# Attention scores with the high and low halves of the keys stacked on the two row halves of the TensorE array

## The chip, the core and the metric

The kernel runs on one core of one Trainium2 chip. The time is the device time of one execution in microseconds, from the first to the last instruction with what lies around them; the shown times are those of repeated runs, and their median counts.

## What is computed

One inference step of a small hybrid network: 128 context tokens and 512 latent tokens of width 1024, two layers. Layer 0 mixes tokens by differential attention, layer 1 by a bidirectional mLSTM; each is followed by a gated ConvFFN. Everything is in 32 bit floats. The change lies in the attention, cut here to what matters (8 heads, two softmax maps m per head, d = DA_DK = 64):

```python
def diff_attend(q, k, v, lam):
    ...
        s = jnp.einsum('bqhmd,bkhmd->bhmqk', qi, k).astype(jnp.float32) * scale
        p = jax.nn.softmax(s, axis=-1)
        a = (p[:, :, 0] - lam * p[:, :, 1]).astype(v.dtype)
        return jnp.einsum('bhqk,bkhd->bqhd', a, v)
```

Context queries see the 128 context keys; latent queries see 128 cached keys and the 512 latent keys, which are rotated (rope) before, as the latent queries are.

## The kernel before

**Precision.** TensorE (PE) multiplies numbers of type fp32r, which are shorter than a float. So every operand is kept as a high part (a cast) and a low part (the float less the high part), and a product is the sum of three: high x high, high x low, low x high. Weights get their high part from ScalarE (ACT, line 1422) and their low part from GpSimd (POOL, line 593); activations get the low part from VectorE (DVE).

**Layout.** The query and key rows of a head are 2 x 64: map 0 on partitions 0 to 63, map 1 on 64 to 127. Qh, Ql (128 x 640: 128 context and 512 latent tokens) and Kh, Kl (128 x 768, with 128 cached keys behind) exist twice, for even and odd heads.

**Scores** (`scores`, L964 to L989). A head has five steps st = 0 to 4; step 0 is the context tile (i = 4), steps 1 to 4 are the four latent query tiles of 128 rows. A latent tile fills `psS`, three banks of 512 columns, with 640 scores of each map: spans of 128 and 512 keys for map 0, of 256 and 384 for map 1. Each span is three matmuls (Qh with Kh, Qh with Kl, Ql with Kh) of 64 rows, so a latent tile has twelve and the context tile six. The spans of 128 (map 0) and 384 (map 1) share a bank: PE waits on its own semaphore `sc_part` ahead of the latter. `psS` exists once: ahead of each tile PE waits for the exponentials of the tile before (`exp_ready`).

**The ring around a tile.** scores (PE) -> `nmax` (DVE: row maximum over psS, L2384, and a small product, L2386) -> `exps` (ACT, L1631) -> `combine` (DVE, L2394 to L2399) -> `turn` (PE: five transposes into psT) -> `turned` (ACT: high part, L1642; DVE: low part Al, L2410) -> values (PE). `psT` exists once too: it holds in turn the transposed tiles, the transposed values of a head (`turn_v`; split by ACT `values_hi` and DVE `values_lo`) and the sums of squares (`rms`, L1025 to L1029). The order in which it is used is a list (`_turn_uses`), and PE waits on `t_free` for the use before.

**The order on each engine** is written out by hand, one function `head` for each. PE puts pieces of the next projections (`qkv`, matmuls into `pj`, L765: pairs of 320 columns, in steps of two) between the attention's steps. At the end of head h PE does: scores(h, 4), 2 pieces, turn(h, 3), 2 pieces, turn_v(h), 2 pieces, rms(h-1) (only h > 0), 1 piece, values_ctx(h), 1 piece, scores(h+1, 0). `rms(h-1)` waits until `values_lo(h)` has freed psT. DVE at the end of head h does: nmax(h, 3), turned(h, 2), rotate("k", h+1), combine(h, 3), nmax(h, 4), turned(h, 3), q_lo(h+1), k_lo(h+1), values_lo(h), and then combine(h, 4). So the low parts of the next head's query and key stand between the last transposed tile and the values. ACT does in the middle of head h: exps(h, 2), q_hi(h+1) (L1668), unit_split(3h+5) (a weight's high part, L1422), turned(h, 2), exps(h, 3), cache_hi(h+1) (the cached keys and values), copy_kv (the value projection), k_hi(h+1) (L1677), turned(h, 3), exps(h, 4), values_hi(h), unit_split(3h+6). POOL's subtraction (L593) follows each unit_split.

The last head prepares no next one; PE fills its gaps with other work (`last_blocks`).

Of the kernel before, what the change touches and what calls it, by code (L numbers as in the profile page):

```python
# [14 lines left out]
P = 128  # L15
# [106 lines left out]
QT = (4, 0, 1, 2, 3)  # L122

# [60 lines left out]
def hybrid_step(nc, a, o):  # L184

    ctx = ExitStack()
    with ctx:
# [62 lines left out]
        with ExitStack() as s:  # L250
# [4 lines left out]
            Qh, Ql, Kh, Kl = ([] for _ in range(4))  # L255
            with ExitStack() as g:
                lwq = sb("lwq", [P, 2, 512], F32, g)
            for k in range(2):
                Qh.append(sb(f"Qh{k}", [P, TP], F32R, s))
                Ql.append(sb(f"Ql{k}", [P, TP], F32R, s))  # L260
            with ExitStack() as g:
                lwk = sb("lwk", [P, 2, 512], F32, g)
            for k in range(2):
                Kh.append(sb(f"Kh{k}", [P, KW], F32R, s))
                Kl.append(sb(f"Kl{k}", [P, KW], F32R, s))
# [9 lines left out]
            ckv = sb("ckv", [P, 2, P], F32, s)  # L275
            sm = sb("sm", [P, 16], F32, s)
            lam = sb("lam", [P, 8], F32, s)
            lamp = sb("lamp", [P, 2, DK], F32, s)
# [462 lines left out]
        def _(pe):  # L741
# [222 lines left out]
            def scores(h, st):  # L964

                idx, par, i = 5 * h + st, h % 2, QT[st]
                if idx > 0:
                    pe.wait_ge(exp_ready, idx)
                if idx == 1:
                    pe.wait_ge(mods_ready, 1)  # L970
                if i == 4:
                    pe.wait_ge(qk_ready, 2 * h + 2)
                    spans = [(0, C0, C0 + CTX, 0), (640, C0, C0 + CTX, 1)]
                    q0 = C0
                else:


                    spans = [(512, L0 + 512, KW, 0), (0, L0, L0 + 512, 0), (1024, L0 + 384, KW, 1), (640, L0, L0 + 384, 1)]
                    q0 = L0 + i * P
                for at, k0, k1, m in spans:  # L980
                    r = slice(DK * m, DK * (m + 1))
                    if i < 4 and at == 640:
                        pe.wait_ge(sc_part, 4 * h + i + 1)
                    for n, (q, kk) in enumerate(((Qh, Kh), (Qh, Kl), (Ql, Kh))):
                        last = mm(psS[:, at:at + k1 - k0], q[par][r, q0:q0 + P], kk[par][r, k0:k1],  # L985
                                  start=(n == 0), stop=(n == 2))
                    if i < 4 and at == 512:
                        last.then_inc(sc_part, 1)
                last.then_inc(sc_done, 1)  # L989
# [423 lines left out]
        def _(act):  # L1413
# [234 lines left out]
            def copy_q(n):  # L1648
                if n > 0:
                    act.wait_ge(qk_ready, 2 * n - 1)  # L1650
                v = _qkv_unit("q", n)
                evac(v // 2, v % 2, h32[0][:, :])
# [13 lines left out]
            def q_hi(n):  # L1666
                act.wait_ge(roped, 2 * n + 1)
                nc.scalar.copy(Qh[n % 2][:, :], h32[0][:, :]).then_inc(qk_hi, 1)  # L1668

            def cache_hi(n):  # L1670
                act.wait_ge(ckv_in, 32 * (n + 1))
                nc.scalar.copy(Kh[n % 2][:, L0 + LAT:KW], ckv[:, 0, :])
                nc.scalar.copy(Vh[n % 2][:, 4, :], ckv[:, 1, :]).then_inc(ckc_hi, 1)

            def k_hi(n):
                act.wait_ge(roped, 2 * n + 2)
                nc.scalar.copy(Kh[n % 2][:, 0:L0 + LAT], h32[1][:, 0:L0 + LAT]).then_inc(qk_hi, 1)  # L1677
# [362 lines left out]
        def _(dve):  # L2040
# [387 lines left out]
            def q_lo(n):  # L2428
                dve.wait_ge(qk_hi, 2 * n + 1)
                tt(Ql[n % 2][:, :], h32[0][:, :], Qh[n % 2][:, :].bitcast(F32), ALU.subtract).then_inc(qk_ready, 1)  # L2430

            def k_lo(n):
                par = n % 2
                dve.wait_ge(ckc_hi, n + 1)
                tt(Kl[par][:, L0 + LAT:KW], ckv[:, 0, :], Kh[par][:, L0 + LAT:KW].bitcast(F32), ALU.subtract)
                tt(Vl[par][:, 4, :], ckv[:, 1, :], Vh[par][:, 4, :].bitcast(F32), ALU.subtract).then_inc(ck_split, 1)
                dve.wait_ge(qk_hi, 2 * n + 2)
                tt(Kl[par][:, 0:L0 + LAT], h32[1][:, 0:L0 + LAT], Kh[par][:, 0:L0 + LAT].bitcast(F32),
                   ALU.subtract).then_inc(qk_ready, 1)
# [457 lines left out]
```

## Time and profile before

| what | value |
|---|---|
| times of 3 runs | 1748.39 us median (1747.43 to 1749.07) |
| profiled execution | 1748.54 us, span from first to last instruction 1746.8 us |
| mean granted TensorE clock | 0.994 of full speed |
| busy in the span | PE 97%, PE weight loads 91%, DVE 63%, ACT 40%, POOL 36% |
| score matmuls (L985) | 432, first at 58.8 us, last at 340.4 us |

The profile's page gives the busy time of each engine; the attention is the stretch from 58 to about 345 us. Matmuls are pipelined: the record of a matmul lasts longer than the array is occupied by it, so the spacing of starts tells its cost, and a busy PE isn't one at its peak. The chain of waits follows the work that ended last back through its releasers; a wait's releaser is inferred from semaphore events.

### The profile page before, as it was taken

The numbers are of one execution on the slowest core, as the hardware profiler recorded it, in microseconds if no ns is written. First come the engines' busy times: TensorE is split into PE (matmuls) and PEld (weight loads), VectorE is DVE, ScalarE is ACT, GpSimd is POOL, SyncE is SP. The second block draws the span as 40 slices with busy tenths as digits, with TensorE's granted clock in tenths as the row PEclk, the third lists the DMA queues.
The fourth block names the chain that finished last, engine by engine and source line by source line (L and its number), as shares of the span: only waits on it lengthen the run. The fifth ranks groups of instructions, "written<-read, shape, count | busy, mean of one in ns | idle before, by whom it ended". The sixth has DMA issues, their size and how long they took to land.

```text
span 1746.8 us, 30132 instructions
## 1 busy us (share of the span) xinstructions
PE 1696.8 (97%) x11450; PEld 1594.1 (91%) x11450; DVE 1097.0 (63%) x1775; ACT 696.4 (40%) x1134; POOL 631.4 (36%) x317
## 2 busy tenths in 40 slices
PE   7999999899999999999999999999999999999996
PEld 4888888598989999889998899998999999999996
DVE  4776777757876515767458554644878861487824
ACT  3455555527332212232246554554463331233324
POOL 2222111356442333323454222124745333333444
PEclk9999999999999999999999999999999999999998
DMA  9322222521444213543221112211212222222221
GB/s 358 136 65 73 62 62 81 207 85 46 190 176 161 97 57 121 183 181 129 83 70 55 64 55 75 71 49 49 91 37 72 72 90 69 70 72 72 86 84 60
DMA packets 59770, 170.97 MB, mean 98 GB/s; under 512 B 7945, under 2 KB 20489, under 8 KB 59665
## 3 DMA queue, kind: packets, MB, share of 16 engines
q1 hardware_dynamic: 51584, 163.33, 26.8%
q10 hardware_dynamic: 8080, 6.18, 1.1%
q8 instruction: 73, 1.20, 0.3%
q14 instruction: 33, 0.26, 0.0%
HBM read 161.07 MB, written 4.74 MB: 95 GB/s over the span
## 4 chain that ended last, share of the span: by engine, by line
PE 74%; DVE 9%; ACT 5%; POOL 4%; issue 4%; DVEq 3%; DMA 1%; ACTq 1%; SPq 0%; POOLq 0%
PE pj L765 58%; POOL wlo L623 3%; PE mO L1280 2%; ACT pr L1631 2%; PE psO L1020 2%; PE pfrow L790 1%; PE psS L985 1%; DVEq L2385 1%; PE st_va L765 1%; POOL ss L637 1%; DVE pr L2399 1%; PE mO L765 1%; PE st_mu L765 1%; DVE sm L2384 1%; PE mS L1236 1%
## 5 line engine op out<-in xcount | busy, mean ns | idle before, releaser
L593 POOL TENSOR_TENSOR wlo<-wraw,whi 128x1024 fp32r<-128x1024 f32 (+1 forms) x116 | 301.9, 2603 | 739.7 <-ACT whi L1422 739.7
L765 PE MATMUL pj<-Hh,whi 128*128 128x320 f32 x2192 | 521.3, 317 | 2.2 <-POOL wlo L623 0.9
L765 PE MATMUL pj<-Hh,wlo 128*128 128x320 f32 x2192 | 504.9, 309 | 0.0
L765 PE MATMUL pj<-Hl,whi 128*128 128x320 f32 x2192 | 502.7, 310 | 0.0
L765 PEld LDWEIGHTS pj<-Hh,whi 128*128 128x128 f32 x2192 | 364.8, 188 | 28.5 <-issue 22.8
L765 PEld LDWEIGHTS pj<-Hh,wlo 128*128 128x128 f32 x2192 | 368.1, 188 | 0.3
L765 PEld LDWEIGHTS pj<-Hl,whi 128*128 128x128 f32 x2192 | 367.5, 188 | 0.4
L1422 ACT CAST whi<-wraw 128x1024 fp32r<-128x1024 f32 (+1 forms) x168 | 187.2, 1114 | 265.2 <-PE pj L765 227.7
L2295 DVE SCALAR_TENSOR_TENSOR fcv<-fus,vec,fcv 128x127 f32<-128x127 f32 (+1 forms) x176 | 206.4, 1214 | 14.4 <-issue 13.8
L1428 ACT COPY fus<-pj 128x640 f32<-128x640 f32 x84 | 58.3, 696 | 382.9 <-PE pj L765 382.9
L2157 DVE SCALAR_TENSOR_TENSOR X<-pj,mods,X 128x128 f32<-128x128 f32 (+5 forms) x114 | 43.1, 434 | 207.4 <-PE pj L765 207.3
L765 PE MATMUL pj<-Gh,whi 128*128 128x320 f32 x704 | 168.4, 310 | 0.8 <-POOL wlo L623 0.8
L765 PE MATMUL pj<-Gh,wlo 128*128 128x320 f32 x704 | 167.4, 308 | 0.0
L765 PE MATMUL pj<-Gl,whi 128*128 128x320 f32 x704 | 167.3, 308 | 0.0
L2298 DVE SCALAR_TENSOR_TENSOR fcv<-fus,vec,fcv 128x127 f32<-128x127 f32 (+1 forms) x176 | 129.1, 774 | 14.4 <-issue 13.8
L2292 DVE TENSOR_SCALAR fcv<-fus,vec 128x640 f32<-128x640 f32 x88 | 61.0, 694 | 111.7 <-ACT fus L1428 111.7
L668 POOL TENSOR_TENSOR wlo<-wraw,whi 128x1024 fp32r<-128x1024 f32 x27 | 68.4, 2534 | 148.7 <-ACT whi L1422 142.1
L765 PEld LDWEIGHTS pj<-Gh,whi 128*128 128x128 f32 x704 | 119.4, 188 | 1.6 <-POOL wlo L623 1.3
L623 POOL TENSOR_TENSOR wlo<-wraw,whi 128x1408 fp32r<-128x1408 f32 (+2 forms) x28 | 85.4, 3049 | 97.4 <-ACT whi L1422 92.9
L765 PEld LDWEIGHTS pj<-Gh,wlo 128*128 128x128 f32 x704 | 119.4, 188 | 0.3
L765 PEld LDWEIGHTS pj<-Gl,whi 128*128 128x128 f32 x704 | 119.5, 188 | 0.0
L2384 DVE TENSOR_REDUCE sm<-psS 128x2 f32<-128x1280 f32 (+1 forms) x40 | 50.9, 1274 | 31.0 <-PE psS L985 30.9
(374 smaller groups left out, 2414.2 us busy)
## 6 DMA issues: line engine op xcount, KB each, us to landing
wraw<-in_w_up SPq DMA_DIRECT2D x84, 512.0 KB, 3.5
fwr<-in_w_ada SPq DMA_DIRECT2D x56, 512.0 KB, 5.7
wraw<-in_w_dn SPq DMA_DIRECT2D x32, 704.0 KB, 4.1
wraw<-in_w_qkv SPq DMA_DIRECT2D x24, 512.0 KB, 3.5
wraw<-in_w_mlin SPq DMA_DIRECT2D x24, 512.0 KB, 3.4
awr<-in_w_ada SPq DMA_DIRECT2D x16, 512.0 KB, 10.4
awr<-in_w_ada SPq DMA_DIRECT2D x16, 256.0 KB, 7.9
wraw<-in_w_wo SPq DMA_DIRECT2D x8, 512.0 KB, 3.5
```

The costliest lines, as they stand in the source:

```text
L593: nc.gpsimd.tensor_tensor(wlo[k][:, 0:width], wraw[k][:, 0:width], whi[k][:, 0:width].bitcast(F32), ALU.subtract).then_inc(w_lo, 1)
L623: nc.gpsimd.tensor_tensor(wlo[k][:, c0:width], wraw[k][:, c0:width], whi[k][:, c0:width].bitcast(F32), ALU.subtract).then_inc(w_lo, 1)
L668: nc.gpsimd.tensor_tensor(wlo[v % 2][:, 0:width], wraw[v % 2][:, 0:width], whi[v % 2][:, 0:width].bitcast(F32), ALU.subtract).then_inc(w_l ...
L765: last = mm(out[:, c, 0:HALF], w, x[:, j, c * HALF:(c + 1) * HALF], start=(j == 0 and n == 0), stop=(j == n_k - 1 and n == 2))
L1020: last = mm(psO[:, :], v_[par][:, c, :], t_[:, c, :], start=(c == 0 and n == 0), stop=(c == 4 and n == 2))
L1422: nc.scalar.copy(whi[k][:, 0:width], wraw[k][:, 0:width]).then_inc(w_hi, 1)
L1428: nc.scalar.copy(dst.rearrange("p (a b) -> p a b", a=2), src[:, :, 0:HALF]).then_inc(pj_copied, 1)
L2157: last = stt(out=x, in0=src[:, bank, c0:c1], scalar=gt, in1=x, op0=ALU.mult, op1=ALU.add)
L2292: ts(c[:, :], f[:, :], tap[1], bias, ALU.mult, ALU.add)
L2295: stt(out=c[:, t0 + 1:t1], in0=f[:, t0:t1 - 1], scalar=tap[0], in1=c[:, t0 + 1:t1], op0=ALU.mult, op1=ALU.add)
L2298: last = stt(out=c[:, t0:t1 - 1], in0=f[:, t0 + 1:t1], scalar=tap[2], in1=c[:, t0:t1 - 1], op0=ALU.mult, op1=ALU.add)
L2384: nc.vector.tensor_reduce(sm[:, 0:2], s_, AX.X, ALU.max)
```

## The change

The scores get a contraction over all 128 rows of the array. For each map m there is now a key tile `Ks[m]` with the high part on the map's own 64 partitions (`OWN[m]`) and the low part on the other 64 (`OTHER[m]`), and a query tile `Qd[m]` with the query's high part on both halves. One `stacked` matmul then gives high x high + high x low; `low_query` (64 rows, the map's own) adds low x high. A latent tile has four of each, in the order tail, right (stacked), tail, right (low), wide (stacked), the wait on `sc_part`, left (stacked), left, wide (low); the context tile has two of each.

The halves have to be written: `q_hi` makes four passes of 64 partitions for one of 128 (two on the own half, then the semaphore `qk_hi`, then two across to the other half), `k_hi` and the keys of `cache_hi` two for one on ACT; `q_lo`, and both subtractions of keys in `k_lo` (writing across to the other half), two for one on DVE. `Ql` exists once and not twice, `Qd` four times; `ckv` and `lamp` lie in unused columns of the weight buffers. `copy_q` waits for the key's low part of the head before, and not the query's.

```diff
--- before.py
+++ after.py
+OWN = (slice(0, DK), slice(DK, 2 * DK))
+OTHER = OWN[::-1]
...
-            Qh, Ql, Kh, Kl = ([] for _ in range(4))
+            Qd, Ks = [], []
...
-                Qh.append(sb(f"Qh{k}", [P, TP], F32R, s))
-                Ql.append(sb(f"Ql{k}", [P, TP], F32R, s))
+                Qd.append([sb(f"Qd{k}{m}", [P, TP], F32R, s) for m in range(2)])
+                if k == 0:
+                    Ql = sb("Ql", [P, TP], F32R, s)
...
-                Kh.append(sb(f"Kh{k}", [P, KW], F32R, s))
-                Kl.append(sb(f"Kl{k}", [P, KW], F32R, s))
+                Ks.append([sb(f"Ks{k}{m}", [P, KW], F32R, s) for m in range(2)])
...
-            ckv = sb("ckv", [P, 2, P], F32, s)
+            ckv = wraw[1][:, D:D + 2 * P].rearrange("p (a k) -> p a k", a=2)
...
-            lamp = sb("lamp", [P, 2, DK], F32, s)
+            lamp = wraw[0][:, D:D + 2 * DK].rearrange("p (a k) -> p a k", a=2)
...
                 if i == 4:
                     pe.wait_ge(qk_ready, 2 * h + 2)
-                    spans = [(0, C0, C0 + CTX, 0), (640, C0, C0 + CTX, 1)]
-                    q0 = C0
+                q0 = C0 if i == 4 else L0 + i * P
+
+                def stacked(at, k0, k1, m):
+                    mm(psS[:, at:at + k1 - k0], Qd[par][m][:, q0:q0 + P], Ks[par][m][:, k0:k1], start=True, stop=False)
+
+                def low_query(at, k0, k1, m):
+                    return mm(psS[:, at:at + k1 - k0], Ql[OWN[m], q0:q0 + P], Ks[par][m][OWN[m], k0:k1], start=False, stop=True)
+
+                if i == 4:
+                    first, second = ((640 * m, C0, C0 + CTX, m) for m in range(2))
+                    stacked(*first)
+                    stacked(*second)
+                    low_query(*first)
+                    last = low_query(*second)
                 else:
-
-
-                    spans = [(512, L0 + 512, KW, 0), (0, L0, L0 + 512, 0), (1024, L0 + 384, KW, 1), (640, L0, L0 + 384, 1)]
-                    q0 = L0 + i * P
-                for at, k0, k1, m in spans:
-                    r = slice(DK * m, DK * (m + 1))
-                    if i < 4 and at == 640:
-                        pe.wait_ge(sc_part, 4 * h + i + 1)
-                    for n, (q, kk) in enumerate(((Qh, Kh), (Qh, Kl), (Ql, Kh))):
-                        last = mm(psS[:, at:at + k1 - k0], q[par][r, q0:q0 + P], kk[par][r, k0:k1],
-                                  start=(n == 0), stop=(n == 2))
-                    if i < 4 and at == 512:
-                        last.then_inc(sc_part, 1)
+                    wide, tail = (0, L0, L0 + 512, 0), (512, L0 + 512, KW, 0)
+                    left, right = (640, L0, L0 + 384, 1), (1024, L0 + 384, KW, 1)
+                    stacked(*tail)
+                    stacked(*right)
+                    low_query(*tail).then_inc(sc_part, 1)
+                    low_query(*right)
+                    stacked(*wide)
+                    pe.wait_ge(sc_part, 4 * h + i + 1)
+                    stacked(*left)
+                    low_query(*left)
+                    last = low_query(*wide)
                 last.then_inc(sc_done, 1)
...
             def copy_q(n):
                 if n > 0:
-                    act.wait_ge(qk_ready, 2 * n - 1)
+                    act.wait_ge(qk_ready, 2 * n)
                 v = _qkv_unit("q", n)
                 evac(v // 2, v % 2, h32[0][:, :])
...
             def q_hi(n):
                 act.wait_ge(roped, 2 * n + 1)
-                nc.scalar.copy(Qh[n % 2][:, :], h32[0][:, :]).then_inc(qk_hi, 1)
+                for m in range(2):
+                    last = nc.scalar.copy(Qd[n % 2][m][OWN[m], :], h32[0][OWN[m], :])
+                last.then_inc(qk_hi, 1)
+                for m in range(2):
+                    nc.scalar.copy(Qd[n % 2][m][OTHER[m], :], h32[0][OWN[m], :])
             def cache_hi(n):
                 act.wait_ge(ckv_in, 32 * (n + 1))
-                nc.scalar.copy(Kh[n % 2][:, L0 + LAT:KW], ckv[:, 0, :])
+                for m in range(2):
+                    nc.scalar.copy(Ks[n % 2][m][OWN[m], L0 + LAT:KW], ckv[OWN[m], 0, :])
                 nc.scalar.copy(Vh[n % 2][:, 4, :], ckv[:, 1, :]).then_inc(ckc_hi, 1)
             def k_hi(n):
                 act.wait_ge(roped, 2 * n + 2)
-                nc.scalar.copy(Kh[n % 2][:, 0:L0 + LAT], h32[1][:, 0:L0 + LAT]).then_inc(qk_hi, 1)
+                for m in range(2):
+                    last = nc.scalar.copy(Ks[n % 2][m][OWN[m], 0:L0 + LAT], h32[1][OWN[m], 0:L0 + LAT])
+                last.then_inc(qk_hi, 1)
             def values_hi(h):
                 act.wait_ge(t_full, USE["v", h] + 1)
...
             def q_lo(n):
                 dve.wait_ge(qk_hi, 2 * n + 1)
-                tt(Ql[n % 2][:, :], h32[0][:, :], Qh[n % 2][:, :].bitcast(F32), ALU.subtract).then_inc(qk_ready, 1)
+                for m in range(2):
+                    r = OWN[m]
+                    last = tt(Ql[r, :], h32[0][r, :], Qd[n % 2][m][r, :].bitcast(F32), ALU.subtract)
+                last.then_inc(qk_ready, 1)
             def k_lo(n):
                 par = n % 2
                 dve.wait_ge(ckc_hi, n + 1)
-                tt(Kl[par][:, L0 + LAT:KW], ckv[:, 0, :], Kh[par][:, L0 + LAT:KW].bitcast(F32), ALU.subtract)
+                for m in range(2):
+                    k_, r = Ks[par][m], OWN[m]
+                    tt(k_[OTHER[m], L0 + LAT:KW], ckv[r, 0, :], k_[r, L0 + LAT:KW].bitcast(F32), ALU.subtract)
                 tt(Vl[par][:, 4, :], ckv[:, 1, :], Vh[par][:, 4, :].bitcast(F32), ALU.subtract).then_inc(ck_split, 1)
                 dve.wait_ge(qk_hi, 2 * n + 2)
-                tt(Kl[par][:, 0:L0 + LAT], h32[1][:, 0:L0 + LAT], Kh[par][:, 0:L0 + LAT].bitcast(F32),
-                   ALU.subtract).then_inc(qk_ready, 1)
+                for m in range(2):
+                    k_, r = Ks[par][m], OWN[m]
+                    last = tt(k_[OTHER[m], 0:L0 + LAT], h32[1][r, 0:L0 + LAT], k_[r, 0:L0 + LAT].bitcast(F32), ALU.subtract)
+                last.then_inc(qk_ready, 1)
```

## Rows read from the trace of the kernel before

**Rows 1.** Windows: stretch, its length, busy us (instructions) by engine, granted clock, DMA
```profile
172.00:210.00 38.00, 37.68 (x256) 33.39 (x256) 27.71 (x48) 20.89 (x43) 7.56 (x4) 1.00 0.22 65
```
**Rows 2.** Chain of waits, head 3: start us, length us, what
```profile
191.22 1.43 PE psS L985 x10
...
195.91 0.82 DVE Al L2410
...
197.87 0.74 DVE Kl L2438
...
199.55 1.31 PE psT L1028 x4
```
**Rows 3.** List of waits, 58 to 350 us: total us, times, longest us
```profile
PE psT L1028 <- DVE Vl L2446: 1.0, 6, 0.2
```
**Rows 4.** Timeline of PE, scores(3, 1): start, length, line, out<-in, count
```profile
172.41 0.39 PE L1020 MATMUL psO<-Ah,Vl 128*128 128x512 f32 x1
172.73 0.32 PE L985 MATMUL psS<-Kh,Qh 64*128 64x128 f32 x1
172.89 0.27 PE L985 MATMUL psS<-Kl,Qh 64*128 64x128 f32 x1
...
173.01 0.55 PE L985 MATMUL psS<-Kh,Qh 64*128 64x256 f32 x2
...
173.83 0.33 PE L985 MATMUL psS<-Kh,Ql 64*128 64x384 f32 x1
174.09 0.55 PE L765 MATMUL pj<-Hh,whi 128*128 128x320 f32 x2
174.48 0.45 PE L765 MATMUL pj<-Hh,wlo 128*128 128x320 f32 x2
174.78 0.45 PE L765 MATMUL pj<-Hl,whi 128*128 128x320 f32 x2
```
**Rows 5.** Groups by line and shape, 55 to 350 us: busy us, mean ns
```profile
L2430 DVE TENSOR_TENSOR Ql<-h32t,Qh 128x640 fp32r<-128x640 f32 x7 | 5.7, 816 | 0.0
```
**Rows 6.** The same view, 800 to 1000 us (the mLSTM's gates)
```profile
L2593 DVE TENSOR_TENSOR O32m<-O32m 36x640 f32<-36x640 f32 x1 | 0.8, 818 | 0.1
...
L1795 ACT ACTIVATE O32m<-mT,gbias 36x640 f32<-36x640 f32 x1 | 0.8, 799 | 0.0
```
**Rows 7.** Timelines of ACT, POOL, DVE and PE in head 3
```profile
185.24 0.72 ACT L1668 CAST Qh<-h32t 128x640 fp32r<-128x640 f32 x1
185.85 1.05 ACT L1422 CAST whi<-wraw 128x1024 fp32r<-128x1024 f32 x1
...
186.98 2.46 POOL L593 TENSOR_TENSOR wlo<-wraw,whi 128x1024 fp32r<-128x1024 f32 x1 [14.65 <-ACT whi L1422]
199.43 2.37 POOL L593 TENSOR_TENSOR wlo<-wraw,whi 128x1024 fp32r<-128x1024 f32 x1 [9.98 <-ACT whi L1422]
...
188.68 0.80 DVE L2386 TENSOR_SCALAR sm<-sm 128x2 f32<-128x2 f32 x1
...
190.12 0.68 DVE L2421 TENSOR_TENSOR sx<-sx,rope 128x512 f32<-128x512 f32 x1
...
193.19 0.89 DVE L2399 SCALAR_TENSOR_TENSOR pr<-pr,sm 128x640 f32<-128x640 f32 x1
...
194.44 0.71 PE L1001 MATMUL psT<-ident,pr 128*128 128x128 f32 x5
```
**Rows 8.** Timelines of DVE and POOL in the first ConvFFN
```profile
473.24 3.17 DVE L2295 SCALAR_TENSOR_TENSOR fcv<-fus,vec,fcv 128x127 f32<-128x127 f32 x2 [0.17 <-issue]
...
473.29 2.57 POOL L668 TENSOR_TENSOR wlo<-wraw,whi 128x1024 fp32r<-128x1024 f32 x1 [1.20 <-ACT whi L1422]
```
**Rows 9.** Timeline of PE, end of head 0
```profile
92.94 0.77 PE L1001 MATMUL psT<-ident,pr 128*128 128x128 f32 x5 [1.36 <-DVE pr L2399]
```
**Rows 10.** Windows, as rows 1, in the last head
```profile
324.00:325.70 1.70, 0.00 (x0) 0.00 (x0) 0.16 (x1) 1.66 (x4) 0.00 (x0) 1.00 0.92 320
328.00:332.00 4.00, 4.00 (x23) 1.61 (x20) 2.87 (x7) 3.06 (x7) 0.27 (x1) 0.57 0.56 213
```

## The prediction

> **What bounds the kernel now.** Counting matmuls would say: PE, the matmul engine. I first cut out the stage that the edit touches, the attention, with one stretch of the windows: in 38 us PE is busy for 37.68, VectorE (DVE) for 27.71, ScalarE (ACT) for 20.89 [rows 1]. A PE that is never idle beside two half idle engines still may not set the time alone, because the engines hand each tile around in a ring: scores, row maximum, exponential, combination, transposes. So second the chain of waits over one steady head, head 3. From the scores of step 1 on (174.2) it runs on DVE and ACT for 17 us, touches PE again at 191.22 for the scores of step 4, and comes back to DVE: the last transposed tile's low part (Al, 195.91), then Ql, Kl and Vl without a gap. PE's rms matmuls (199.55) can only follow Vl, and from there PE is the chain up to the next scores of step 1 [rows 2]. Third the list of waits: in six heads of eight these rms matmuls are released by Vl, up to 0.2 us after PE ran dry [rows 3]. So DVE has no slack between Al and Vl, and PE next to none before them. Two things matter: how long a score tile takes, and every microsecond of DVE between Al and Vl.
>
> **The score matmuls.** Twelve become eight, but the instruction stream shows what the twelve cost [rows 4]. The matmuls of map 0 (upper 64 rows of the array) and of map 1 (lower 64) already run beside each other: map 1's 256 columns start at 173.01, while map 0 is at work. Each half streams 3 x 640 = 1920 columns. Afterwards a stacked matmul takes the whole array, 1280 columns, and the low queries, which can still pair up, add max(128, 256) + max(512, 384) = 768: 2048. The saved third was hidden by the other half.
>
> Then the edges. The last full-array matmul ahead of the tile starts at 172.41 and lasts 0.23 by its columns (0.30 for twice 320 at 174.48), so the tile was due at 172.64. It comes at 172.73, and its second step 0.16 later where 0.11 is usual for weights of 128 columns: 0.15 to get in. The last score matmul (384 columns, 0.18) starts at 173.83 and leaves the array at 174.01; the projection starts at 174.09, and its second step comes 0.39 later against 0.30 for the third: 0.18 to get out. In all 172.64 to 174.19, 1.55 us. The new tile goes full, halves, full, halves, full: two such pairs of edges. In the spacings of rows 4: tail 0.11, right 0.12, in 0.15, pair 0.15, out 0.18, wide 0.23, left 0.18, in 0.15, pair 0.26, out 0.18, together 1.71: **0.16 us more per latent tile**, not less. Bounds: 0.13 less than now if the second pair of edges costs nothing, 0.4 more if the low queries run one after the other; I take 0.16, since both edges of the trace have the gap. The wait on sc_part is covered by the wide matmul, which stands between the short low query and it. The context tile changes three double steps for a stacked pair and a low pair between the same two edges: nothing, within 0.05.
>
> The Trainium skill says of this, in TensorEngine Tiling (Array Packing), Key Properties, that changing the tiling mode, and not just the tile, drains the array. By that rule the 0.33 us of edges is owed a second time, as I took it; if the gaps came from the semaphore wait ahead of the tile instead, the lower bound would hold, some 0.3 us per head less. The way out has no wait in front of it and shows the larger gap, so the trace sides with the rule.
>
> **The split of queries and keys.** Full-height instructions become pairs of half-height ones. Does a half cost half? A DVE subtraction of 128 x 640 takes 816 ns [rows 5], one of 36 x 640 takes 818, and an ACT pass of 36 x 640 takes 799 though it reads partitions from 64 on and writes them from 0 on [rows 6]. **Height is free, so each half costs the whole**, and the shift across partitions nothing on ACT; on DVE no row has one, and I take nothing too.
> DVE, between Al and Vl: one more Kl, 0.74, one more Ql, the same size, and one more cache part. From Al's end (195.91 + 0.82) to Kl (197.87) lie one Ql and two cache parts, 1.14, so a part is 0.20 [rows 2]. **1.67 us more on the chain in each head.**
> ACT: three more query passes and one more key pass, 0.61 apart (185.24 to 185.85 [rows 7]), and a cache pass of some 0.2: 2.6 us of an engine that idles 17 in 38. Key and cache passes lie in idle time ahead of turned(h, 3). The query passes stand ahead of the head's weight cast (185.85), which so comes 1.83 later, and with it GpSimd's subtraction (POOL), which starts 1.13 after the cast, and what DVE does beside it. PE needs those weights after the scores of step 4, 192.6, and has them at 191.4. The new wait of copy_q (2n for 2n - 1) is for a subtraction that ends before Vl, so before PE goes on: nothing. ckv and lamp move in memory and queue nowhere; the DMAs stay.
>
> **What DVE and POOL do to each other.** While POOL subtracts (2.4 us), DVE instructions from memory stand: L2386, on two numbers a row, takes 0.80 and ends with POOL [rows 7]. And where POOL comes while DVE works on a pair of them, it goes in between: POOL at 473.29, DVE's pair from 473.24 stretched to 3.17 [rows 8]. So I work out where POOL's two subtractions of a head fall.
> First: the chain behind step 1 is 0.16 later; four query passes from 185.40, the cast at 187.84, POOL 188.97 to 191.37. L2386 comes at 188.68 now, and 0.16 (the chain) to 0.32 (two score tiles in PE's order) later: 188.84 to 189.0, a tie; I take it as ahead. But then rotate("k") (L2421, 190.12) stands until 191.37 and its first step ends 1.2 late; the combination, done at 194.08 now, ends 195.3, and the transposes start at 195.35 in place of 194.44 [rows 7]: **Al is 0.9 us late**.
> Second: this POOL start follows the value transposes, which wait for Al: 199.43, 3.52 after Al [rows 2, 7]. The new order is Al, two Ql, two cache parts, V, two Kl; the second Kl would start 0.82 + 1.46 + 0.40 + 0.20 + 0.74 = 3.6 after Al. POOL comes during the first Kl and goes in between, as in rows 8. The second Kl is done at some 6.6, Vl at 7.5, and PE starts at 7.65 after Al where it is 3.64 now: **4.0 us late** in place of 1.67.
>
> **Sum.** A head with an rms behind it: 0.9 + 4.0 = 4.9 us, six of them: 29.4. Head 0 has no rms; PE there waits for the combination [rows 9], which already contains its POOL stall: of the 4.0 about 1.9 are left, 2.8 with the 0.9. The last head prepares nothing: two tiles on its chain, 0.3. The prologue's 1.67 lies under the 16 matmuls of ada_block(5) and the projection ahead of the first scores: nothing, or 1.7 once. Together 32.5 on the profiled execution's 1748.54 us (1746.8 span and 1.7 around it; the median of the runs is 1748.39): **1781 us**.
>
> **Rivals.**
> *POOL waits.* If the second Kl gets in ahead of POOL (0.1 us by my count), a head costs 0.9 + 1.67 = 2.6: six are 15.4, head 0 some 1.6, with the last head 17.3: 1766; with the lower bound of the tile 1762. Rows 8 speak against it.
> *L2386 is caught as well.* Then the exponentials of step 3 wait until 191.4, the scores of step 4 start at 193.2 and Al comes 2.1 late: 1.2 more in seven heads, 1789. The tie of rows 7 decides.
> *The clock falls.* PE stands some 4 us per head in the forecast. In the last head it stands from 324 to 325.7, and over the 4 us from 328 on the granted clock is 0.57, a mean of the levels 1.2 and 2.4 GHz: 4 x 0.43 = 1.7 us of PE lost [rows 10]. At 1.5 each in six heads 1790, with the former 1798. Against it: in steady heads PE's work on either side of the gap is dense.
> *It does what it says.* A half costs half, so DVE adds nothing, and the tile loses a third of its 1.43 us (172.73 to 174.16), 0.48, at two places of the chain: 0.96 x 7 = 6.7 less, 1742. The price of a half-height DVE instruction decides: at x of a full one DVE adds (2x - 1) x 1.67, and the gain lives below x = 0.79. Rows 6 say x = 1; then even a full third leaves 0.7 us a head too much, 1753.
>
> **Chances.** Forecast 0.38, POOL waits 0.20, L2386 caught 0.17, the clock (with or without that) 0.12, it does what it says 0.04; 0.04 for within 0.2% (3.5 us, about what a measurement tells from no change), with x in between; 0.05 for the 1753. The range takes in all but the ends: 1758 to 1799. Faster 0.04, same 0.04, slower 0.92.
>
> **What would show it.** Right: Ql and Kl halves of 0.82 us each; PE's gap ahead of L1028 grown from 0.2 to some 4 us, released by Vl; a second Kl of 3 us beside POOL; a head's first POOL start 2 us later after its scores; score tiles of 1.6 to 1.7 us with gaps of 0.1 inside. Wrong: halves of 0.4 us; score tiles near 1.0; a PE that goes into rms without a wait.

## The result

The changed kernel takes 1797.43 us (median of 4 runs, 1796.47 to 1797.93), the kernel before beside it 1748.08: a ratio of 1.0285, 95% interval 1.0273 to 1.0297. It is slower by 49 us; the forecast was slower by 32.5. The profiled span is 1796.2 us against 1746.8, and the difference arises in the attention: each head takes some 7.6 us more from one rms to the next, and the last rms of the attention comes 51.6 us later (405.70 against 354.14). Some 2 us come back behind it, 1.5 of them where the kernel before runs at a granted clock of 0.83 from 1190 to 1200 us; this profile has 1.00 over the same work, 1240 to 1250.

The windows of the changed kernel, columns as in [rows 1], over a stretch of the same length:

```profile
172.00:210.00 38.00, 33.36 (x193) 28.76 (x194) 25.06 (x43) 18.63 (x36) 5.22 (x2) 0.91 0.16 48
```
PE was busy for 37.68 there; now it stands for 4.6 us, and what it does runs at a granted clock of 0.91. The list of waits from 58 to 420 us (total, times, longest):

```profile
PE psT L1041 <- DVE Vl L2473: 27.8, 6, 4.6
PE psT L1014 <- DVE pr L2419: 3.8, 8, 1.2
PE psO L1024 <- DVE Vl L2473: 3.7, 1, 3.7
```
The first line is that of [rows 3], 1.0 us in six heads before, 27.8 now. The third is head 0, which has no rms: there the values of the context tile wait for Vl.

The timelines of DVE, POOL and PE at the end of head 3 (compare [rows 2, 7]):

```profile
218.07 0.83 DVE L2430 TENSOR_TENSOR Al<-psT,Ah 128x640 fp32r<-128x640 f32 x1
218.81 1.64 DVE L2452 TENSOR_TENSOR Ql<-h32t,Qd 64x640 fp32r<-64x640 f32 x2
220.49 0.59 DVE L2460 TENSOR_TENSOR Ks<-wraw,Ks 64x128 fp32r<-64x128 f32 x2
...
221.41 3.70 DVE L2465 TENSOR_TENSOR Ks<-h32t,Ks 64x640 fp32r<-64x640 f32 x2
225.14 0.69 DVE L2472 TENSOR_TENSOR Vl<-psT,Vh 128x512 fp32r<-128x512 f32 x1
...
221.60 2.84 POOL L596 TENSOR_TENSOR wlo<-wraw,whi 128x1024 fp32r<-128x1024 f32 x1 [8.94 <-ACT whi L1435]
...
226.18 1.82 PE L1041 MATMUL psT<-ss,ones 128*128 128x320 f32 x4 [4.63 <-DVE Vl L2473]
```
The two halves of the key are one group of 3.70 us: 0.82 for the first, then POOL up to 224.44, then the second. The rms follows Al by 8.11 us, where it was 3.64 [rows 2].

The groups by line and shape over 58 to 410 us (busy us, mean ns), against [rows 5, 6]:

```profile
L2465 DVE TENSOR_TENSOR Ks<-h32t,Ks 64x640 fp32r<-64x640 f32 x14 | 25.8, 1844 | 0.3
L2452 DVE TENSOR_TENSOR Ql<-h32t,Qd 64x640 fp32r<-64x640 f32 x14 | 11.4, 815 | 0.1
L1682 ACT CAST Qd<-h32t 64x640 fp32r<-64x640 f32 x14 | 10.1, 720 | 0.1
```
A half takes 815 ns on DVE, a whole 816; 720 ns on ACT, a whole 0.72 us [rows 7]. The 1844 is the mean of halves with and without POOL in between.

PE's timeline over a latent tile, as [rows 4]:

```profile
193.13 0.39 PE L1033 MATMUL psO<-Ah,Vl 128*128 128x512 f32 x1
193.36 0.39 PE L979 MATMUL psS<-Ks,Qd 128*128 128x128 f32 x2
193.68 0.38 PE L982 MATMUL psS<-Ks,Ql 64*128 64x128 f32 x2
194.00 0.67 PE L979 MATMUL psS<-Ks,Qd 128*128 128x512 f32 x2
194.60 0.50 PE L982 MATMUL psS<-Ks,Ql 64*128 64x384 f32 x2
195.03 0.56 PE L768 MATMUL pj<-Hh,whi 128*128 128x320 f32 x2
195.42 0.46 PE L768 MATMUL pj<-Hh,wlo 128*128 128x320 f32 x2
```
From its start to the next projection it takes 1.67 us, against 1.36 before (172.73 to 174.09). From the last matmul ahead of it, which takes in the way into the tile, it is 1.90 (193.13 to 195.03) against 1.68 (172.41 to 174.09): 0.22 us more.

The windows of 1 us behind the gap:

```profile
225.00:226.00 1.00, 0.00 (x0) 0.00 (x0) 0.97 (x4) 0.00 (x0) 0.00 (x0) 1.00 0.62 111
226.00:227.00 1.00, 0.82 (x3) 0.69 (x4) 0.85 (x5) 0.00 (x0) 0.00 (x0) 0.93 0.88 348
227.00:228.00 1.00, 1.00 (x3) 0.61 (x3) 0.76 (x1) 0.00 (x0) 0.00 (x0) 0.50 0.17 66
...
230.00:231.00 1.00, 1.00 (x7) 1.00 (x7) 0.00 (x0) 0.27 (x1) 0.00 (x0) 0.87 0.00 0
```
After 4.6 us without a matmul the clock stands at 0.50 for three microseconds, the lower of the two levels, 1.2 GHz for 2.4: 1.7 us of PE lost in this head (0.07 + 3 x 0.50 + 0.13).

### The profile page after: what moved, and what is told of

The parts are those of the page before. It is cut to its first block, busy times and chain, and to the rows that moved or that the text cites. A ratio compares the mean times of both kernels' runs of the same rounds, so it can differ in the third digit from the quotient of the medians.

```text
span 1796.2 us, 29908 instructions
## 1 busy us (share of the span) xinstructions
PE 1717.1 (96%) x11306; PEld 1598.5 (89%) x11306; DVE 1123.5 (63%) x1799; ACT 722.9 (40%) x1174; POOL 632.4 (35%) x317
## 4 chain that ended last, share of the span: by engine, by line
PE 74%; DVE 8%; ACT 5%; POOL 4%; issue 4%; DVEq 3%; DMA 1%; ACTq 1%; SPq 0%; POOLq 0%
PE pj L768 59%; POOL wlo L626 3%; PE mO L1293 2%; PE psO L1033 2%; PE pfrow L793 1%; DVEq L2415 1%; PE st_va L768 1%; POOL ss L640 1%; PE psS L979 1%; PE psT L1041 1%; PE psS L982 1%; PE mO L768 1%; PE st_mu L768 1%; ACT whi L1435 1%; PE mS L1249 1%
## 5 line engine op out<-in xcount | busy, mean ns | idle before, releaser
L2315 DVE SCALAR_TENSOR_TENSOR fcv<-fus,vec,fcv 128x127 f32<-128x127 f32 (+1 forms) x176 | 205.7, 1209 | 14.9 <-issue 14.3
L2318 DVE SCALAR_TENSOR_TENSOR fcv<-fus,vec,fcv 128x127 f32<-128x127 f32 (+1 forms) x176 | 134.5, 805 | 14.3 <-issue 13.7
## 6 DMA issues: line engine op xcount, KB each, us to landing
awr<-in_w_ada SPq DMA_DIRECT2D x16, 512.0 KB, 10.3
```

The source lines that it names most:

```text
L2315: stt(out=c[:, t0 + 1:t1], in0=f[:, t0:t1 - 1], scalar=tap[0], in1=c[:, t0 + 1:t1], op0=ALU.mult, op1=ALU.add)
L2318: last = stt(out=c[:, t0:t1 - 1], in0=f[:, t0 + 1:t1], scalar=tap[2], in1=c[:, t0:t1 - 1], op0=ALU.mult, op1=ALU.add)
```

## The experiments

All ratios are to the kernel before, run beside each on the same chip (medians 1746.7 to 1747.1 us). First come the parts, then the mechanism, then its price. "Period" is the time from one head's rms to the next in a steady head: 36.7 us before, 44.1 to 44.9 in the changed kernel (mean 44.4).

### The tile alone

```diff
-                for m in range(2):
-                    last = nc.scalar.copy(Qd[n % 2][m][OWN[m], :], h32[0][OWN[m], :])
-                last.then_inc(qk_hi, 1)
-                for m in range(2):
-                    nc.scalar.copy(Qd[n % 2][m][OTHER[m], :], h32[0][OWN[m], :])
+                nc.scalar.copy(Qd[n % 2][0][:, :], h32[0][:, :]).then_inc(qk_hi, 1)
...
```
The same for the keys and on DVE: every split is one whole-height instruction again, the eight matmuls stay.

> The eight matmuls of a tile as in the changed kernel, but queries and keys split by one full-height instruction each, as before the change; the scores are then not the reference's (map 1 multiplies the query's high part with the key's low part). Theory 'the splits cost it': a latent tile is 0.16 to 0.2 us longer than before, twice on the chain of a head and once or twice more in PE's order, so 1749.5 to 1753 us. Rival 'the tile gains, the splits hide it': a third of the matmuls gone shows, 1741 to 1746. Rival 'the tile costs it': the edges between full array and halves are worth most of the 49 us, over 1770.

Measured: 1751.94 us (1749.48 to 1755.12), ratio 1.0026, interval 1.0015 to 1.0037; a period of 37.25 us, and the clock at 1.00 up to the last head. So the eight matmuls by themselves gain nothing: they cost 0.6 us a head. From the last matmul ahead of a tile to the next projection, the tiles of steps 1 to 3 take 1.89, 1.96 and 2.03 us, against 1.68, 1.75 and 1.75 before; that of step 4, ahead of which PE stood for the exponentials before, takes 1.97 against 1.95.

### The splits alone

```diff
+                    for n, q in enumerate((Qd[par][m], Qd[par][m], Ql)):
+                        last = mm(psS[:, at:at + k1 - k0], q[r, q0:q0 + P], Ks[par][m][r, k0:k1], start=(n == 0), stop=(n == 2))
```
The twelve 64-row matmuls again, on the new tiles, whose halves are written as in the changed kernel.

> The half-height splits of the changed kernel, but twelve matmuls of 64 rows a tile, in the order before the change (the second of a span reads the key's high part once more in place of the low part, so the scores are not the reference's). Theory 'the splits cost it': nearly all of the 49 us stays, 1793 to 1797. Rival 'the tile costs it': 1750 to 1765. If the tile gains, more than the changed kernel's 1797.4.

Measured: 1796.17 us, ratio 1.0277 (1.0253 to 1.0301), and the same wait of PE as in the changed kernel, 27.8 us in six heads, 4.6 the longest. The loss is the splits.

### Halves on one engine only

ScalarE's copies in halves, VectorE's whole:

```diff
+                for m in range(2):
+                    last = nc.scalar.copy(Ks[n % 2][0][OWN[m], 0:L0 + LAT], h32[1][OWN[m], 0:L0 + LAT])
...
+                tt(Ks[par][1][:, 0:L0 + LAT], h32[1][:, 0:L0 + LAT], Ks[par][0][:, 0:L0 + LAT].bitcast(F32),
+                   ALU.subtract).then_inc(qk_ready, 1)
```

> The kernel of the tile alone (VectorE's splits whole) with ScalarE's copies in halves as the changed kernel has them: two halves and two more for the query, two for the key, two for the cached keys; both halves of the high key go to one tile and VectorE's whole-height difference to the other, so the scores are not the reference's. It splits the cost of the halves between the two engines. Theory A (VectorE's sequence ahead of Vl is the main cost, ScalarE only makes Al some 1.4 us late per head): 1751.9 + 6 x 1.4 = 1760 us, range 1756 to 1766, no idle stretch over 1 us ahead of rms, the clock 1.00. Theory B (ScalarE's halves carry half the loss or more, through Ah, the casts and POOL): 1772 us or more.

VectorE's in halves, ScalarE's whole:

```diff
+                for m in range(2):
+                    k_, r = Ks[par], OWN[m]
+                    last = tt(k_[1][r, 0:L0 + LAT], h32[1][r, 0:L0 + LAT], k_[0][r, 0:L0 + LAT].bitcast(F32), ALU.subtract)
```

> The kernel of the tile alone with VectorE's three low parts in halves (query, cached keys, keys: two instructions of 64 rows each in place of one of 128), ScalarE's copies whole. Each half stays on its own rows, where the changed kernel moves the key's halves to the other rows; the scores are not the reference's. Theory A (the two engines' halves add up, and what counts on VectorE is that two halves take twice the time of the whole and let POOL's split in between; the move to other rows costs nothing by itself): what ScalarE's halves do not explain, 1797.4 - (1758.2 - 1751.9) = 1791 us, range 1785 to 1796, with rms 8.1 us behind Al and 4.6 us of PE idle ahead of it. Theory B (the move across the rows, or the meeting of both engines' halves, is what costs): 1775 us or less, with the two key halves 1.65 us together.

Measured: ScalarE's halves 1758.15 us (ratio 1.0057, 1.0042 to 1.0072), as expected; a period of 38.06, 0.8 above the tile alone, and the rms 3.64 us behind Al as before. VectorE's halves 1797.5 us (1.0283, 1.0266 to 1.03), as much as the whole change. So VectorE's halves carry the loss, 45.6 us over the tile alone, and the expectation that the two add up (1791) was wrong by 6: ScalarE's 6 us are there only when VectorE's halves are not. Their timeline shows the same key halves, though here no half moves to other rows:

```profile
220.12 3.69 DVE L2458 TENSOR_TENSOR Ks<-h32t,Ks 64x640 fp32r<-64x640 f32 x2
223.85 0.69 DVE L2465 TENSOR_TENSOR Vl<-psT,Vh 128x512 fp32r<-128x512 f32 x1
```
The move to other rows costs nothing. Why the two engines' shares don't add shows in the stretches of a head. From the tile of step 1 to Al of step 4 it takes 23.91 us here and 24.71 in the changed kernel, so ScalarE's halves do make Al 0.8 us later there too. But from the rms to the next tile of step 1 it takes 12.0 to 12.7 us here, against 11.3 to 12.1: behind the gap of head 3 the granted clock is 0.50 from 224 to 230 us here, in the changed kernel from 227 to 230. What Al wins, the low clock takes back; why it falls earlier here is not shown.

### POOL waits, and PE kept busy

```diff
+                if v % 3 == 0 and v >= 6:
+                    pool.wait_ge(qk_ready, 2 * (v // 3))
+                split_one(v, D)
```

> The changed kernel, with GpSimd's second weight subtraction of a head waiting until the next head's key is split (one wait more on GpSimd, nothing else). Theory: the second Kl half (start to Vl 2.88 us) stands behind GpSimd; it falls to 0.85, rms starts some 6.1 us after Al in place of 8.1, 2.0 in six heads: 1785; if the shorter gap leaves PE's clock up, another 1.5 in each: 1776. Rival 'writing across the halves is what makes the second Kl slow': it keeps its length and the time stays at 1797.

Measured: 1774.88 us (1.0156, 1.013 to 1.0181), 22.5 us less and close to the 1776 of the theory with the clock; a period of 40.47 us, the rms 6.06 us behind Al, PE's wait 2.6 us a head, the clock at 1.00 but for one window. The timelines of DVE, POOL and PE:

```profile
210.91 1.65 DVE L2468 TENSOR_TENSOR Ks<-h32t,Ks 64x640 fp32r<-64x640 f32 x2
...
213.62 1.38 DVE L2419 TENSOR_TENSOR sm<-sm,lam 128x1 f32<-128x1 f32 x1
...
215.54 0.88 DVE L2422 SCALAR_TENSOR_TENSOR pr<-pr,sm 128x640 f32<-128x640 f32 x1
...
212.64 2.35 POOL L671 TENSOR_TENSOR wlo<-wraw,whi 128x1024 fp32r<-128x1024 f32 x1 [10.49 <-DVE Ks L2468]
...
217.38 0.77 PE L1017 MATMUL psT<-ident,pr 128*128 128x128 f32 x5
```
The two key halves take 1.65, so 2.0 of the 3.70 us were POOL's. The split now catches the next two-operand step of DVE, the product ahead of `pr`, and there it costs nothing: pr is done at 216.4, and PE comes to its transposes at 217.4. From the rms to the tile of step 1 it is 9.70 us, as with the tile alone.

```diff
+                    pe.wait_ge(o_free, 2 * h)
+                    for _ in range(18):
+                        mm(psO[:, :], Hh[:, 0, 0:P], Hh[:, 0, 0:512], start=True, stop=True)
```
This puts 18 matmuls of no use into PE's gap ahead of rms, in the changed kernel.

> The changed kernel, with 18 more matmuls of 512 columns (4.1 us, into a bank that is overwritten later) in PE's gap ahead of rms. Theory: the gap of 4.6 us is followed by about 3.5 us at a granted clock of 0.5, worth 1.7 us in each of six heads; with the gap filled the clock stays at 1.00: 1786 to 1788. Rival 'the low clock lies beside other waits and costs nothing': 1797.

Measured: from head 2 on the clock is 1.00, a period is 42.57 us, and the last rms of the attention comes 10.3 us earlier: 1.7 us in six heads, what the windows above give for the clock. The time falls by less, to 1791.56 us (1788.42 to 1794.69; 1.0251, 1.0219 to 1.0283). The profiled run is the slower of the two, and 7 us of its lead on the changed kernel go behind the attention: 4.4 at 1040 to 1070 us, where PE waits 3.9 us for DVE in the mLSTM and its clock falls, and the 2 that the changed kernel's profile gets back. Why DVE is late there I didn't follow up.

### Where the halves stand

Only the place of one line is changed, then of one more:

```diff
                 q_lo(h + 1)
+                values_lo(h)
                 k_lo(h + 1)
-                values_lo(h)
```

> The changed kernel with one line moved: VectorE takes the low part of the values (two instructions, 0.69 and 0.28 us) between the query's low halves and the key's low halves, in place of behind the key's. No instruction is added or taken away. Theory A (the halves cost because they stand ahead of Vl, on which the matmul that overwrites psT waits; neither their own busy time nor their lateness matters): rms falls back to some 3.7 us behind Al of step 4 (8.1 in the changed kernel), the idle stretch of PE of 4.6 us goes, the low clock behind it goes with it (1.7 us), and head 0's 3.7 us too; a head from rms to rms 38.3 us in place of 44.5; 1797.4 - 6 x 6.2 - 3.7 = 1756 us, range 1751 to 1762. Theory B (the work only comes late elsewhere: the key's low halves then hold up the scores of the next head, or combine of step 4, by what was saved): at most a third of it comes back, 1783 to 1797 us.

```diff
                 k_hi(h + 1)
+                q_twice(h + 1)
                 turned(h, 3)
```
(`q_twice` is the second pair of copies of `q_hi`; head 0 keeps the old place.)

> The kernel with the values first, and one more thing moved: ScalarE makes the query's second copy (two halves, 1.46 us) behind the key's high halves, where it idled 1.28 us before Ah of step 4, in place of ahead of the cast that POOL's first split waits on and of Ah of step 3. Theory A (the 1.4 us from the scores to Al come from ScalarE's queue and from POOL's split meeting the rotation of the key because the cast ended late): Ah of step 3 comes some 1.4 us earlier, the rotation's first product takes 0.7 to 0.9 us in place of 1.68, a head takes 37.0 to 37.5 us; 1750 to 1754 us, what the tile alone took (1751.9). Theory B (the copy is not what makes Al late, or its new place delays Ah of step 4 by what was saved): as the kernel with the values first, within 3 us.

Measured: values first 1788.96 us (1.024, 1.0224 to 1.0255): my theory fell, 8.5 us came back and not 41. The gap ahead of rms is gone, and the waits of PE from 60 to 420 us say where it went:

```profile
PE psT L1014 <- DVE pr L2419: 10.6, 15, 1.1
PE psS L979 <- DVE Ks L2465: 10.4, 7, 2.7
```
PE reaches the next head's context scores some 3 us after the start of rms, and needs the key there; behind it, the transposes need pr. With the second copy moved too it is 1778.67 us (1.0175, 1.0161 to 1.0188): the rotation's first product takes 0.68 again (1.68 in the changed kernel), but a period is still 40.9 and not the 37.0 to 37.5 of theory A. Al comes no earlier, 24.95 us after the tile of step 1 against 24.69 with the values first: POOL's first split now catches the small product of step 3 (1.42 us for 0.17), and the copies in their new place stand ahead of Ah of step 4. What came back, by the trace, is the clock, 1.00 from head 3 on: from the rms to the next tile of step 1 it takes 12.4 us, with the values first 13.8 to 15.0. DVE and POOL in that kernel:

```profile
204.92 1.42 DVE L2411 TENSOR_SCALAR sm<-sm 128x2 f32<-128x2 f32 x1
...
203.91 2.40 POOL L596 TENSOR_TENSOR wlo<-wraw,whi 128x1024 fp32r<-128x1024 f32 x1 [15.77 <-ACT whi L1435]
...
216.90 2.67 DVE L2465 TENSOR_TENSOR Ks<-wraw,Ks 64x128 fp32r<-64x128 f32 x2
...
216.97 2.45 POOL L596 TENSOR_TENSOR wlo<-wraw,whi 128x1024 fp32r<-128x1024 f32 x1 [10.66 <-ACT whi L1435]
```
POOL's second split now catches the cached keys. Next, POOL's split is held there too, as above:

> The kernel with values first and the query's second copy moved, and POOL's second split of a head held until the key's low halves are done. Theory A (what is left of the loss there is the split that catches the low halves of the cached keys, 2.67 us in place of 0.6, and so makes the key late for the next head's context scores, on which PE waits 1.3 us, with the combination behind it 1.1 us later than before): the cached halves take 0.6, the waits of psS on Ks go, a head takes 38 to 38.8 us in place of 40.9; 1778.7 - 6 x 2.5 - 1 = 1763 us, range 1758 to 1768. Theory B (the held split comes too late for its matmuls, or the key's halves are late without the collision): 1774 us or more.

Measured: 1779.16 us (1.0188, 1.0171 to 1.0205), no gain: theory A fell again. The cached halves take 0.59, PE doesn't wait for the key but for 0.6 us once, and the collision has moved on once more:

```profile
217.16 2.18 DVE L2424 TENSOR_TENSOR sm<-sm,lam 128x1 f32<-128x1 f32 x1
219.27 0.54 DVE L2425 TENSOR_SCALAR pr<-pr,sm 128x640 f32<-128x640 f32 x1
...
216.97 2.36 POOL L671 TENSOR_TENSOR wlo<-wraw,whi 128x1024 fp32r<-128x1024 f32 x1 [13.24 <-DVE Ks L2473]
...
220.82 0.77 PE L1017 MATMUL psT<-ident,pr 128*128 128x128 f32 x5 [2.58 <-DVE pr L2427]
```
A product of 0.16 us takes 2.18, and PE stands 2.58 us for pr. So in this order the path isn't Al to Vl but Al to pr, and it is one unbroken sequence of DVE: where POOL comes into it, its end is 2 us later.

### The price of the collision

The kernel with both moved, and the kernel before, each with POOL's second split on 8 columns of 1024:

```diff
+                split_one(v, 8 if v % 3 == 0 and v >= 6 else D)
```

> The kernel with values first and the query's second copy moved, in which POOL's second split of each head works on 8 columns of the 1024 (so that the low part of that weight is stale, and the result is not the reference's): no POOL instruction of 2.4 us lies beside VectorE's low parts. It prices what the collision costs there. Theory A (the split costs the 2 us that it takes from VectorE's sequence from Al to pr of step 4 wherever it stands in it, since PE waits for the end of that sequence): the cached halves take 0.6, PE's waits on Ks and on pr behind rms go (2.4 us a head), 1778.7 - 7 x 2.2 = 1763 us, range 1759 to 1767. Theory B (the plain durations of the halves carry the loss, the collision is hidden beside PE's work): 1774 us or more.

> The kernel before with the same cut: POOL's second split of each head on 8 columns, the low part of that weight stale. In the kernel before this split catches L2396 behind the values' low parts (2.26 us in place of 0.16, at 199.55). Theory A (there it costs nothing, since pr ends at 203.2 and PE comes to its transposes at 203.4 anyway): the time of the kernel before within 0.2%, 1744 to 1750 us; with the run beside it, the split costs some 2 us a head in the changed kernel's order and none in that of before. Theory B (it costs 2 us a head in both): 1735 us or less.

Measured: 1762.78 us (1.0095, 1.0074 to 1.0117), 15.9 us less than with the split, 2.3 in each of seven heads, with a period of 38.80; and 1746.18 us (0.9996, 0.9986 to 1.0005), no change. The same POOL instruction costs 16 us beside the halves, in this order, and nothing in the kernel before. There, too, it stops DVE for 2 us, as its timeline shows:

```profile
199.55 2.26 DVE L2396 TENSOR_TENSOR sm<-sm,lam 128x1 f32<-128x1 f32 x1
...
202.35 0.88 DVE L2399 SCALAR_TENSOR_TENSOR pr<-pr,sm 128x640 f32<-128x640 f32 x1
...
203.37 0.77 PE L1001 MATMUL psT<-ident,pr 128*128 128x128 f32 x5
```
and without the split:

```profile
199.63 0.16 DVE L2397 TENSOR_TENSOR sm<-sm,lam 128x1 f32<-128x1 f32 x1
...
200.33 0.89 DVE L2400 SCALAR_TENSOR_TENSOR pr<-pr,sm 128x640 f32<-128x640 f32 x1
```
Before, pr ends at 203.2, and PE comes to its transposes at 203.4 on its own. POOL's 2.1 us used up the slack of that sequence to within 0.2 us, so the first added half had nowhere to go.

### The twelve matmuls in another order

The kernel before with the two maps' matmuls in turn, in the context tile too, nothing else:

```diff
+                    for n in range(3):
+                        done = term(n, *tail)
+                        term(n, *right)
+                    done.then_inc(sc_part, 1)
...
+                    for n in (1, 2):
+                        term(n, *left)
+                        last = term(n, *wide)
```

> The kernel before with only its twelve 64-row matmuls of a latent tile put in another order: those of the two maps in turn (three pairs tail beside right, then wide beside left), nothing else. In the kernel before the three of a map follow one another on the same row half. Theory A (two matmuls on different row halves run beside each other, as the two pairs of step 4 in the rows of before and the pairs in the changed kernel do, so that the interleaved order gains what the present one leaves): 0.1 to 0.2 us less a latent tile, 28 tiles, 2.8 to 5.6 us in all where PE sets the pace: 1741 to 1745 us. Theory B (the stretch around the scores is set by what PE does next or by the other engines, or the halves already overlap as far as they can): within 0.1%, 1745.5 to 1749 us.

Measured: 1746.44 us (1.0000, 0.9991 to 1.0009). A tile takes 1.32 us from its first score to the projection (185.69 to 187.01), against 1.35 in the kernel before (185.40 to 186.75): the halves overlapped already. No version that I ran beats the kernel before.

## Why the prediction was right, and where it was off

The time lies inside the range, close to its upper end. That end stood for the clock together with a caught L2386; the clock fell, L2386 was missed, and head 0, Al and the spacing of the halves made up the rest. The direction and the mechanism were forecast; that the number is still in the range is in part luck.

**The cause: right.** Vl released PE, the gap grew to 4.6 us (forecast some 4), POOL went in between the two key halves, the small product of [rows 7] was missed by POOL's first split (L2406 took 0.17) and the rotation was caught (L2441, 1.68).

**The tile: the sign right, the size and the place too small.** I had 0.16 us more per latent tile; it is 0.21 to 0.28 in steps 1 to 3, and nothing in step 4, where PE waited before. I let it count at two places of the chain in the last head and inside Al's lateness elsewhere. Alone it costs 5 us, 0.6 a head. The Trainium skill's rule that a change of the tiling mode drains the array (TensorEngine Tiling (Array Packing), Key Properties) agrees with the sign of this, as [rows 4] did.

**Height is free: right; two halves at the spacing of wholes: wrong.** I spaced the added Ql and Kl by 0.74, the step from one whole subtraction to the next. The two halves of a pair don't overlap at all: they take 1.64 together, and the next step starts 1.68 behind their start (218.81 to 220.49). ACT's pairs take 1.45, where I had 0.61 for each pass. So the first key half started 3.34 us behind Al and not 2.88. POOL came 3.53 behind it (forecast 3.52), and the rms 8.11 (forecast 7.65): the whole difference of 0.46 is this term.

**Al 0.9 us late: it was 1.4** (24.94 us from the last matmul ahead of the tile of step 1 to Al, 23.50 before). The four query passes take 2.96 us up to the weight's cast (206.16 to 209.12), and not 2.44: halves at the spacing of wholes once more. So POOL's first split, and the rotation that stands beside it, end some 0.5 us later than I counted. The passes also stand ahead of Ah of step 3 on ACT, as the chain of waits of the changed kernel shows:

```profile
206.27 0.61 ACT Qd L1682
206.89 0.72 ACT Qd L1682
207.64 0.72 ACT Qd L1685
208.38 0.73 ACT Qd L1685
209.12 1.05 ACT whi L1435
210.16 0.60 ACT Ah L1655
210.78 0.82 DVE Al L2430
```
I had counted ACT as idle for 17 us in 38 and didn't name this Ah. But its Al is done at 211.6, and POOL, for which the rotation stands, at 212.7:

```profile
211.53 1.68 DVE L2441 TENSOR_TENSOR sx<-sx,rope 128x512 f32<-128x512 f32 x1
...
210.24 2.42 POOL L596 TENSOR_TENSOR wlo<-wraw,whi 128x1024 fp32r<-128x1024 f32 x1 [17.21 <-ACT whi L1435]
```

**The clock: the step that failed.** I gave its fall a chance of 0.12, as "PE's work on either side of the gap is dense". It fell in every steady head and cost 1.7 us each (priced at 1.5): the run with PE kept busy had 10.3 us of it back at the end of the attention, of some 17 that were missing. It is the largest part of the miss. Dense work around the gap was no reason; [rows 10] was the case to go by.

**Head 0: sized from the wrong wait.** I took 2.8 us from the combination, where PE waited before [rows 9]. It now waits 3.7 us for Vl ahead of that, at the context values, with Al's lateness still to come on top: from its first score to the first score of head 1 it takes 38.7 us against 32.3, 6.4 more.

**POOL waits: a rival priced too low.** Made on purpose, it gives 1774.9 and not 1766. The collision that it moves to the product ahead of pr costs nothing there; what I had too small is the halves themselves: the rms comes 6.06 us behind Al and not 5.31 (3.64 + 1.67), and Al is later by the 0.5 above. One head also has a low clock (a period of 42.28). My reading that only the stretch from Al to Vl has no slack held for the order of the changed kernel; the kernels with moved lines show that pr stands close behind, and holds PE up once Vl doesn't. In the Trainium skill (SBUF — State Buffer, section "SBUF: two separate sides") the ports that DVE and POOL share are an exclusive lock: whoever starts first keeps them for the whole instruction, where the DVE instruction reads two operands there or runs in a mode that uses two ports. The places where the second split was seen agree: a two-operand step of DVE stood for 2.0 to 2.1 us at the key halves, the cached keys and the product ahead of pr, for 1.2 where it met the split's end, and POOL's split of 2.4 us took 2.84 where it came during the first key half. The small product that the first split held (1.42 us for 0.17) is no such two-operand step; whether it ran in such a mode no run here shows.

**Where the 49 us are, by differences of medians:** the tile 5; the query's second copy in its old place 10 (values first against both moved), which by the trace is the low clock, as Al comes no earlier without it; the values behind the key 8.5; POOL's collision 16; the plain length of the halves and what remains 11 (1762.8 against 1751.9). These depend on the order in which the parts are taken out, as ScalarE's share shows (6 alone, 0 on top), and POOL's (16 here; 22.5 with the clock where it was taken out of the changed kernel itself).

## What to carry to other kernels

A split by partitions doubles an elementwise instruction's cost, so a matmul saving that needs it has to be weighed against the engine that does the splitting, in the stage where it stands. Follow that engine's unbroken sequence to the last result that PE waits for, not to the first: a collision that costs nothing sits in slack, and after a small addition the same collision can cost its full length. Moving it helps only where the result behind it still comes before PE does: pr did with POOL waiting in the changed kernel (216.4 against 217.4), and didn't with the values first. And two matmul streams on different row halves that already overlap leave nothing for stacking them to save.

## What was not expected of the hardware

- Two neighbouring whole-height subtractions on DVE start 0.73 us apart though each lasts 0.82, and two ACT copies 0.61 apart at 0.72; pairs on opposite partition halves start 0.82 to 0.85 and 0.72 to 0.74 apart. What keeps the second half from starting early was not tested.
- Whether the clock falls isn't told by the length of the gap alone. With the values first PE stands 1.28 and 1.10 us near 222 and 224, and the clock goes to 0.50:

```profile
222.00:224.00 2.00, 0.67 (x4) 0.48 (x4) 1.88 (x5) 0.69 (x1) 0.00 (x0) 1.00 0.82 260
224.00:226.00 2.00, 0.96 (x6) 0.97 (x7) 1.85 (x5) 0.00 (x0) 0.00 (x0) 0.82 0.14 33
226.00:228.00 2.00, 2.00 (x9) 2.00 (x9) 1.35 (x5) 1.80 (x6) 0.00 (x0) 0.50 0.18 41
```
With the second copy moved as well it stands 1.29 and 1.10 us in the same places, and the clock stays at 1.00 from head 3 on, after 0.92 and 0.96 in the heads before. What decides between them stays open.
